# Second expert weights in rows of 8 KB, and activations turned by every second column

## What is computed

```
def expert_rows(args):
    xe, e = args
    hh = xe @ w1[e] + b1[e]                      # w1[e]: 1024 x 2048
    glu = jnp.minimum(hh[:, :D_FF], SWIGLU_LIMIT)
    lin = jnp.clip(hh[:, D_FF:], -SWIGLU_LIMIT, SWIGLU_LIMIT)
    act = glu * jax.nn.sigmoid(SWIGLU_ALPHA * glu) * (lin + 1.0)
    return act @ w2[e] + b2[e]                   # w2[e]: 1024 x 1024
```

## Time and profile before

| | us |
|---|---|
| median of 3 runs | 1456.1 |
| lowest, highest | 1455.57, 1456.11 |
| the profiled execution | 1456.45 |
| its span, first to last instruction | 1454.6 |
| PE busy in it | 1427.3 |
| DVE busy in it | 1315.1 |
| ACT busy in it | 1104.3 |
| POOL busy in it | 440.1 |

### The profile page before, as it was taken

How to read it: one execution, slowest core, us unless ns; L and a number is a source line. 1 busy time by engine, 2 the same in 40 slices (tenths; PEclk the granted TensorE clock), 3 DMA queues, 4 the chain that set the end, 5 groups by cost and what they waited for, 6 DMA issues and landing times.

```text
span 1454.6 us, 22413 instructions
## 1 busy us (share of the span) xinstructions
PE 1427.3 (98%) x7078; PEld 1161.0 (80%) x7078; DVE 1315.1 (90%) x1528; ACT 1104.3 (76%) x1349; POOL 440.1 (30%) x178
## 2 busy tenths in 40 slices
PE   9999999999999999999999999999999999999996
PEld 7777787787888888888888888888888888888884
DVE  5778766689999999999999999999999999999997
ACT  5668554467888888888888888888888888888885
POOL 3000000051433333444333334444333333334321
PEclk9999999999999999999999999999999999999998
DMA  8021022469999999999999999999999999999963
GB/s 258 12 80 59 30 88 72 107 234 392 409 392 399 399 390 388 383 384 380 380 379 389 374 380 386 374 382 378 368 385 380 378 380 378 369 385 381 377 241 127
DMA packets 98317, 451.88 MB, mean 311 GB/s; under 512 B 11427, under 2 KB 23715, under 8 KB 65506
## 3 DMA queue, kind: packets, MB, share of 16 engines
q1 hardware_dynamic: 90962, 434.68, 77.7%
q0 software_dynamic: 7312, 16.63, 5.0%
HBM read 440.99 MB, written 18.48 MB: 316 GB/s over the span
## 4 chain that ended last, share of the span: by engine, by line
PE 86%; DVE 9%; ACT 3%; issue 2%; DMA 0%; SPq 0%; DVEq 0%; ACTq 0%
PE zpair L2243 48%; PE bank L2243 23%; PE bank L1942 2%; PE bank L1830 2%; PE bank L1832 2%; PE bank L1831 2%; DVE stage_lo L1237 2%; PE bank L2201 1%; PE bank L2193 1%; DVE lbuf L1317 1%; PE zpair L2212 1%; DVE pt_lo L1326 1%; DVE lbuf L1313 0%; DVE cols L1334 0%; PE zpair L1830 0%
## 5 line engine op out<-in xcount | busy, mean ns | idle before, releaser
L1237 DVE TENSOR_TENSOR stage_lo<-ring,stage_hi 128x1024 fp32r<-128x1024 f32 x796 | 945.5, 1221 | 37.9 <-ACT stage_hi L801 10.3
L801 ACT CAST stage_hi<-ring 128x1024 fp32r<-128x1024 f32 x796 | 828.2, 1054 | 168.4 <-PE zpair L2243 133.8
L676 POOL DMA_INDIRECT x_scratch<-qk,sidx x31 | 250.5, 8079 | 264.0 <-ACT qk L1120 264.0
L2243 PE MATMUL zpair<-stage_hi,act_hi 128*128 128x512 f32 x1024 | 322.6, 396 | 0.3 <-DVE act_lo L1642 0.3
L2243 PE MATMUL zpair<-stage_hi,act_lo 128*128 128x512 f32 x1024 | 316.8, 391 | 0.0
L2243 PE MATMUL zpair<-stage_lo,act_hi 128*128 128x512 f32 x1024 | 315.9, 390 | 0.5 <-DVE stage_lo L1237 0.5
L2243 PEld LDWEIGHTS zpair<-stage_lo,act_hi 128*128 128x128 f32 x1024 | 192.0, 188 | 42.8 <-DVE stage_lo L1237 1.4
L2243 PEld LDWEIGHTS zpair<-stage_hi,act_lo 128*128 128x128 f32 x1024 | 192.2, 188 | 41.1
L2243 PEld LDWEIGHTS zpair<-stage_hi,act_hi 128*128 128x128 f32 x1024 | 187.2, 188 | 43.0 <-issue 7.3
L2243 PE MATMUL bank<-stage_hi,act_hi 128*128 128x512 f32 x510 | 159.9, 395 | 0.0
L2243 PE MATMUL bank<-stage_lo,act_hi 128*128 128x512 f32 x510 | 157.1, 389 | 0.0
(11 more groups left out here) (310 smaller groups left out, 1432.9 us busy)
## 6 DMA issues: line engine op xcount, KB each, us to landing
ring<-in_w SPq DMA_DIRECT2D x384, 1024.0 KB, 9.2
ring<-in_w_in SPq DMA_DIRECT2D x12, 1024.0 KB, 5.3
ring<-in_w_out SPq DMA_DIRECT2D x4, 1024.0 KB, 4.8
xs_all<-in_x SPq DMA_DIRECT2D x4, 512.0 KB, 6.8
ring<-in_x SPq DMA_DIRECT2D x4, 512.0 KB, 3.6
tn_scratch<-qk SPq DMA_DIRECT2D x4, 512.0 KB, 2.8
x_scratch<-ring SPq DMA_DIRECT2D x4, 512.0 KB, 4.2
ring<-x_scratch SPq DMA_DIRECT2D x4, 512.0 KB, 5.8
```

The lines of the kernel that those rows point to most:

```text
L676: nc.gpsimd.indirect_dma_start(out=x2_d[:, :], out_offset=bass.IndirectOffsetOnAxis(ap=sidx[:, 0:1], axis=0), in_=yout, in_offset=None, bo ...
L801: nc.scalar.copy(dst, src).then_inc(split_hi, 1)
L1237: nc.vector.tensor_tensor(dst, src, hi_ap.bitcast(F32), ALU.subtract).then_inc(split_lo, 1)
L2243: mm = pe.matmul(bank[b0 + h][:], w[:, k, :], m[:, j % STAGES, h * BANK:(h + 1) * BANK], start=start and w is T_hi and m is stage_hi, stop ...
```

## The change

The second weights' rows are dealt to partitions in pairs. Of each 256 rows, partition `p` gets rows `2p` and `2p+1`, which are neighbours in memory, and takes them as one run of 8 KB. The slot's first half then holds the even rows and the second half the odd ones; they are still used as pieces `2c` and `2c+1`. So that they meet their activations, `turn_a` takes for block `k` of 256 columns the even ones (`k` even) or the odd ones (`k` odd): 128 floats with a stride of two. Nothing else is changed; loads, waits, instructions and their order on every engine are as many and the same as before.

```
-    w2_d = w2[0].rearrange("e (k p) n -> e k p n", p=P)
+    w2_d = w2[0].rearrange("e (c p j) n -> e c p (j n)", p=P, j=2)
...
-                    src = w2_d[e_w2, k:k + 2].rearrange("k p n -> p k n") if isinstance(e_w2, int) else \
-                        w2_d[bass.ds(e_w2, 1), k:k + 2].rearrange("e k p n -> p (e k) n")
-                    sp.dma_start(slot(z).rearrange("p (k n) -> p k n", k=2), src).then_inc(full[z], 16)
+                    src = w2_d[e_w2, k // 2] if isinstance(e_w2, int) else \
+                        w2_d[bass.ds(e_w2, 1), k // 2].rearrange("e p n -> p (e n)")
+                    sp.dma_start(slot(z), src).then_inc(full[z], 16)
...
-                sp.dma_start(slot(z).rearrange("p (k n) -> p k n", k=2),
-                             w2_d[E - 1, k:k + 2].rearrange("k p n -> p k n")).then_inc(full[z], 16)
+                sp.dma_start(slot(z), w2_d[E - 1, k // 2]).then_inc(full[z], 16)
...
             def turn_a(t):
                 pe.wait_ge(act_made, t + 1)
+                columns = lin.rearrange("t (c p j) -> t c j p", p=P, j=2)
                 for k in range(KT):
-                    mm = pe.transpose(bank[6 + k // 4][:, k % 4 * CAP:(k % 4 + 1) * CAP], lin[:, k * P:(k + 1) * P], identF[0:CAP, 0:CAP])
+                    mm = pe.transpose(bank[6 + k // 4][:, k % 4 * CAP:(k % 4 + 1) * CAP], columns[:, k // 2, k % 2, :], identF[0:CAP, 0:CAP])
```

More of the change, by code:

```diff
@@ L589, in _ @@
                     sp.wait_ge(*REST.freed(OVER - 1, c - KT))
-                    sp.dma_start(slot(z).rearrange("p (k n) -> p k n", k=2),
-                                 w2_d[bass.ds(el, 1), k:k + 2].rearrange("e k p n -> p (e k) n")).then_inc(full[z], 16)
+                    sp.dma_start(slot(z), w2_d[bass.ds(el, 1), k // 2].rearrange("e p n -> p (e n)")).then_inc(full[z], 16)
                 sp.wait_ge(all_scattered, 1)
```

## The result

| | before, us | after, us |
|---|---|---|
| median of 5 runs | 1455.99 | 1464.7 |
| lowest, highest | 1455.42, 1456.11 | 1464.34, 1465.39 |
| the profiled execution | 1456.45 | 1464.54 |
| its span | 1454.6 | 1462.7 |

The change made the kernel slower by a factor of 1.0061, 95% interval 1.0046 to 1.0076, that is 8.7 us: clear of the 0.2% named above, and 1.2 us beyond the upper end of the range.

What follows compares the result with a forecast made beforehand. PE was taken to bound the kernel at 34.66 us per expert. Loads 0, turn 0 and SP's issues 0 left the runs' median unchanged at 1456.1 us, with a range of 1454.8 to 1463.5.

Steps and rivals of the forecast that it cites:

- What bounds the kernel: Expert stage: PE, full and almost never waiting, sets the pace at 34.66 us per expert; loads follow freed slots.
- The loads at 0: Second weights' loads: 16,384 fewer packets, at most 38 us less latency, all beside PE, so cost 0.
- The turn at 0: Eight activation transposes per expert on PE: the strided weight load stays hidden under the transpose ahead, cost 0.
- the nearest row: Profile row of the contiguous transpose weight load, same shape and kind, 140 ns, taken as covered; basis for cost 0.
- the cover: On PE, time under the preceding transpose that hides a weight load; transposes start 82 ns apart, its size unknown.
- The row at 192 ns: Router's plain fp32 matmuls: 128x128 weight load of 192 ns sets their distance, 0.111 us; upper bound 6.5 us.
- The first rival: PE's eight transposes: strided load loses its cover; +6.5 us, 1462.6, far bound 1506.8; chance 0.19, 0.16 near the first.
- 50.7 us: Far bound for the turn on PE: each load takes twice its 140 ns and overlaps nothing, over 256 transposes.
- the POOL queue: Gathers and scatters sharing DMA engines: longer packets delay them, 1488 at one us beyond the spare; chance 0.02.
- lighter DMA traffic: PE's expert matmuls: fewer packets shorten each by 1 ns, 4.6 us in all, 1451.5; chance 0.04.

Runs made afterwards that it cites:

- loads_only: The change with the turn of activations left contiguous, so only the loads of second weights are altered: 1455.96 us, ratio to the kernel before 1.0004.
- both_turns: The kernel before with a stride of two in both turns of each expert, activations and gathered rows: 1473.15 us, ratio 1.0122.
- covered4: The kernel before with every weight load of the second product, under 512-column matmuls, read at a stride of four: 1470.71 us, ratio 1.0106.
- wide: The kernel before with a contiguous turn of activations of 128 moving columns instead of 96: 1461.22 us, ratio 1.0035.

## Why the prediction was wrong

**What bounds the kernel**: right. PE's period moved the time: 32 x 0.283 us, less a wait of 0.27 us at the end. Nothing else is seen to have moved it.

**The loads at 0**: right in its cost: 81,933 packets, no effect (loads_only, 1.0004 with 1 inside its interval). That the landing would come down to the first weights' level because of the rows is not shown: it came down as far in kernels that kept the old rows (median 7.7 us in both_turns, 7.9 in covered4). After the change the queues moved 378 to 398 GB/s and PE waited for no load; the limit of about 358 GB/s in the Trainium skill ("DMA: Bandwidth & Descriptors", Specifications) is passed here too, with one core at work; what holds with its neighbour at work, no run here shows.

**The turn at 0**: this is the step that failed. The prediction put it as: the nearest row is the contiguous load, which is covered, so take 0. That the contiguous load is covered was right (wide shows it), but how deep the cover is had been left open, and the stride was then booked at the price of a row that has no stride. The runs showed a load of 218 ns in its place, which sets a distance of its own, 120 ns where the moving columns had set 82, and 0.283 us per expert. The row at 192 ns, called another kind of operation, was the better guide.

**What spoke for it**: for the load of a transpose with 96 moving columns the traces show +78 ns at a stride of two and the same +78 ns at four; for the load of split operands +5 ns at two and +118 at four. The Trainium skill ("Advanced Engine Details and Errata", SBUF Cachelines) has it that two hits on a 16-byte line are enough to hide the memory's latency. Transposes contradict it twice: a stride of two floats, with two hits, is not free, and a stride of four, with one, costs no more. With split operands its direction is right. The prediction said that no run showed this rule here, and gave 0.73 to the free turn, for which it had this rule and a cover of unknown depth.

**The first rival**: the right mechanism, with a chance of 0.16 near its price, mis-sized: 6.5 us were forecast and 8.7 measured. The estimate had 29 ns for each of seven distances, 0.20 us per turn, and these grew by 0.22, so the 192 ns row was nearly the right price for them; that the first load stays hidden was right too. What it put at nothing is what follows the eighth transpose: 0.04 us to the next matmul and 0.02 us in the second product. 0.22 + 0.04 + 0.02 = 0.28 us and 32 of them make 9.1 us; less PE's wait of 0.27 us that the last turn used up, 8.8 us would have come out. The range ended at this rival's estimate plus 0.9 us, with no room for the size of a term that no row had bounded from above except at 50.7 us.

**The other rivals** fell: the POOL queue and lighter DMA traffic show nothing in the period of loads_only, and the 8 KB rows did go as single packets.

## What to carry to other kernels

Where the tensor engine has no idle time, an operand's layout is a cost of its own: a stride in a stationary operand was paid on that engine here, in part only where something longer streamed above the load, but never with nothing. If columns must be dealt, let the operation that already moves the data out of PSUM do it; here that was free. And a faster transfer is worth nothing while its issuer waits for slots: read that wait before the packet sizes.

## What the runs showed of the hardware

- The weight load of an fp32 transpose, 128 columns: 140 ns contiguous, at both starts that were tried; 218 ns at a stride of two or four floats with 96 moving columns, 209 at two with 128; 207 ns at eight. With 96 moving columns, eight of them lengthen an expert by 0.283, 0.267 and 0.217 us at strides of two, four and eight.
- The weight load of a split operand under 512 moving columns: 188 ns contiguous, 193 at two, 306 at four; an expert's 48 such matmuls lengthen its period by 0.293 and 0.493 us. Matmul starts lie 226.7, 233.3 and 235.0 ns apart; the second matmul behind the turn of the gathered rows starts 318, 322 and 436 ns after the first.
- Transposes with 128 moving columns start 109 ns apart contiguous, 120 at a stride of two; with 96, 82 and 120.
- A 1 MB load takes the issuing queue 378 ns with two rows of 4 KB per partition, 333 ns with one of 8 KB; a difference in landing is not shown.
- DVE reads PSUM at a stride of two floats as fast as neighbours: 678 ns for 96 x 512 in both.
